# Reordering both ends of the expert loop: router on unscaled x1, selection per token tile, three early splits, the last down product pulled forward

## The chip, the cores and the metric

The kernel runs on one core of a Trainium2 chip. A core has a matrix engine (TensorE: PE for its matmuls, PEld for its weight loads), VectorE (DVE), ScalarE (ACT), GpSimd (POOL) and SyncE (SP), which here only issues DMAs. The five run their own instruction streams and meet only at semaphores: an instruction waits until a semaphore has reached a value, and another instruction's end raises it. PSUM is the accumulator memory that TensorE writes, in eight banks of 2 KB for each of 128 partitions; SBUF is the working memory. The metric is the device time of one execution in microseconds (us), lower is better, and the median over runs is compared.

## The reference, cut to what matters

One layer: attention of two kinds, a residual, then a mixture of experts with another residual. The change touches only the second half:

```python
x1 = x + concat(y_a, y_b) @ w_o                 # 512 tokens x 1024
h  = rms_norm(x1, g_ffn)                        # x1 * rsqrt(mean(x1^2) + eps) * g_ffn
logits = h @ w_router + b_router                # 32 experts
top_vals, top_idx = top_k(logits, 4)
gates = softmax(top_vals)
# for each expert e, for the tokens that chose it (at most 128 are worked on at once):
gu  = xb @ w_gu[e] + b_gu[e]                    # 1024 -> 2048
glu = min(gu[:, :1024], 7); lin = clip(gu[:, 1024:], -7, 7)
act = glu * sigmoid(1.702 * glu) * (lin + 1)
y   = (act @ w_down[e] + b_down[e]) * gate      # 1024 -> 1024
out = x1 + sum over the experts of y, each row added to its token's row
```

## The kernel before, in words

Tokens are worked on in four tiles of 128 (`T` = 4). Everything up to the router follows `PLAN`, one list of steps that every engine walks through in the same order, each doing its part of a step. In `attend(n)` the table `late` places the steps that follow a token tile's attention, by how many attention units later they come: `post` (x1 = output projection + x, DVE L1283; its squares on ACT, L965), `post_mean` and the power on POOL, `post_norm` (h2, DVE L1295), `turn_h2` (PE transposes h2 in eight 128x128 blocks, ACT and DVE copy one half each out of PSUM), `route` (eight matmuls with the router weights, then bias, maximum and index on DVE, L1308 to L1312). x1 is written to `out`, h2 to a table `hd` in device memory, both by SP.

After the plan comes the selection for all four tiles at once on DVE (L1316 to L1332): a one-hot of the four choices (`one`, 512 elements a partition), its sum over the choices (`selm`), a bf16 copy (`selb`, semaphore `picked`); PE turns it into running counts (`rank_ps`); DVE makes `rank`, each token's place in each expert's list, and `cnt`, the longest list, and then raises `routed`. `slots` (ACT L990 and L993) makes the 0/1 matrix of tokens against places for expert j as relu(1 - |place - rank|); `find` (PE) makes the list of token numbers from it, `slot_rows` (DVE) stores it as `idx`, and POOL gathers the rows of h2 with an indirect DMA (`gather`, L788) into `xg`. `spread_gates` (DVE) and `find_gates` (PE) do the same for the gates.

The expert loop computes in fp32 by splitting each number in a high and a low part and adding three products. A *chunk* is 1 MB of expert weights; each expert has eight for the first product (`NG` = 8) and four for the second (`ND` = 4). SP loads a chunk into one of eight buffers (`RAW` = 8) as soon as that buffer's last chunk has been split; `split_hi` (ACT L629) and `split_lo` (DVE L634) write its two parts to one of four places (`HL` = 4); `chunk_products` (PE L1627) runs twelve 512-column matmuls on it and raises `chunk_used`, for which the split four chunks later waits. Around them, for expert i: `turn_x` (PE transposes the gathered rows, ACT and DVE write high and low part of `xT`), `gate_up` (bias matmuls that start four PSUM banks, then eight chunks), `sigmoid` and `lin` (ACT L1026 and DVE L1383, both on those banks), `activate` (DVE L1390 and L1394, semaphore `act_ok`), `turn_a` (transposes the result, written as `aT`), `down` (bias matmuls, then four chunks), `y_rows` (ACT L1034 scales by the gates into the one buffer `ysb`), `scatter` (POOL L797, an indirect DMA that adds rows to `out`). While `gate_up(i)` runs, the work of expert i-1 is finished: PE runs `gate_up(i)`, `turn_x(i+1)`, `down(i-1)`.

The same loop body stands a second time inside `more_rounds`, for experts with more than 128 tokens. With these inputs it isn't entered, but each engine still loads `cnt` and steps three times through the loop's head before it reaches the end of the program.

The order on each engine is the order in which the code is written. The two ends that the change touches are the functions `act_round`, `dve_round`, `pe_round` and `pool_round`.

## Time and profile before

| | |
|---|---|
| median of 3 runs | 1646.47 us (1644.99 to 1647.39) |
| the profiled execution | 1646.24 us, span 1644.5 us |
| busy in that span | PE 1519.8 us (92%), DVE 1310.6 (80%), ACT 1113.0 (68%), POOL 212.8 (13%) |
| mean granted TensorE clock | 0.955 of full speed |
| matmuls of the expert chunks | 3072 + 1536 of 394 ns each |
| weight loads of the experts | 256 + 128 of 1024 KB, 7.4 and 7.0 us from issue to landing |

The span runs from the first to the last instruction; 1.7 us of the execution lie around it. The end of a matmul in the trace is modelled, and matmuls overlap, so a mean of 394 ns doesn't say how closely they follow each other; the start times of a run of matmuls do. Times named below as "at 402.4" are microseconds from the start of the span.

### The profile page before, as it was taken

How to read it: one execution, taken by the hardware profiler on the slowest of the kernel's cores; microseconds unless marked ns; L12 is line 12 of the kernel's file. 1: busy time of each engine (PE TensorE's matmuls, PEld its weight loads, DVE VectorE, ACT ScalarE, POOL GpSimd, SP SyncE). 2: the span in 40 equal slices, each digit the busy share in tenths (PEclk: the TensorE clock that was granted, in tenths of full speed). 3: DMA queues.
4: the chain of work that ended last, by engine and by line, in shares of the span. 5: the costliest groups of instructions: out<-in, count | busy, mean ns of one | idle time of the engine just before them, and what ended most of it. 6: DMA issues, size and time to landing. Idle time of an engine off the chain costs nothing.

```text
span 1644.5 us, 19287 instructions
## 1 busy us (share of the span) xinstructions
PE 1519.8 (92%) x7379; PEld 1227.3 (75%) x7382; DVE 1310.6 (80%) x1249; ACT 1113.0 (68%) x1225; POOL 212.8 (13%) x156
## 2 busy tenths in 40 slices
PE   6888668996799999999999999999999999999994
PEld 5776556775577888887887888888887888888883
DVE  4668847544599888888898888988898888888992
ACT  5544364552577777777777777777777777777771
POOL 1734301001000100001000100001000110001000
PEclk9999958996799999999999999999999999999997
DMA  6312011118579999999989999999999999999960
GB/s 186 90 52 64 1 57 47 39 39 302 186 298 355 358 357 354 359 356 363 357 333 361 360 349 350 362 354 363 360 338 353 358 352 355 354 353 363 360 254 14
DMA packets 97632, 446.62 MB, mean 272 GB/s; under 512 B 17264, under 2 KB 18416, under 8 KB 64688
## 3 DMA queue, kind: packets, MB, share of 16 engines
q1 hardware_dynamic: 87264, 428.39, 68.8%
q0 software_dynamic: 9216, 16.81, 4.0%
q8 instruction: 61, 1.00, 0.2%
q14 instruction: 51, 0.42, 0.1%
q10 hardware_dynamic: 1040, 0.00, 0.0%
HBM read 440.95 MB, written 20.97 MB: 281 GB/s over the span
## 4 chain that ended last, share of the span: by engine, by line
PE 83%; DVE 10%; ACT 3%; issue 2%; DMA 0%; POOL 0%; SPq 0%; ACTq 0%; DVEq 0%; POOLq 0%
PE ps L1627 64%; PE ps L1636 2%; PE ps L1447 2%; PE ps L1454 2%; PE ps L1448 2%; PE ps L1449 2%; PE ps L1606 2%; PE ps L1614 2%; DVE work L1191 1%; PE ps L1535 1%; PE ps L1653 1%; DVE top L1190 1%; DVE whl L634 1%; DVE rp L1148 1%; DVE ss L1127 1%
## 5 line engine op out<-in xcount | busy, mean ns | idle before, releaser
L634 DVE TENSOR_TENSOR whl<-wraw,whl 128x2048 fp32r<-128x2048 f32 x383 | 863.6, 2289 | 131.6 <-ACT whl L629 127.0
L629 ACT ACTIVATE whl<-wraw 128x2048 fp32r<-128x2048 f32 x384 | 735.8, 1917 | 243.4 <-PE ps L1627 243.3
L1627 PE MATMUL ps<-whl,xT 128*128 128x512 f32 x3072 | 726.5, 394 | 0.2 <-DVE whl L634 0.2
L1627 PEld LDWEIGHTS ps<-whl,xT 128*128 128x128 f32 x3072 | 572.5, 189 | 128.3 <-issue 11.8
L1627 PE MATMUL ps<-whl,aT 128*128 128x512 f32 x1536 | 360.3, 394 | 1.8 <-DVE aT L1376 1.8
L1627 PEld LDWEIGHTS ps<-whl,aT 128*128 128x128 f32 x1536 | 287.9, 189 | 72.3 <-issue 11.2
L797 POOL DMA_INDIRECT out_dram<-ysb,idx x32 | 74.1, 2315 | 551.5 <-ACT ysb L1034 551.5
L788 POOL DMA_INDIRECT xg<-h_rows,idx x32 | 33.6, 1051 | 560.9 <-DVE idx L1356 560.5
L1447 PE MATMUL ps<-W,HT 128*128 128x512 f32 (+1 forms) x184 | 72.7, 395 | 1.7 <-DVE HT L1103 1.7
L1448 PE MATMUL ps<-W,HT 128*128 128x512 f32 (+1 forms) x184 | 70.5, 383 | 0.0
L1449 PE MATMUL ps<-W,HT 128*128 128x512 f32 (+1 forms) x184 | 70.4, 383 | 0.0
L911 ACT ACTIVATE raw<-ps,nmax 128x256 f32<-128x256 f32 (+2 forms) x48 | 27.8, 580 | 55.6 <-DVE nmax L1204 55.6
L1204 DVE TENSOR_REDUCE nmax<-ps 128x1 f32<-128x128 f32 (+3 forms) x64 | 31.0, 487 | 31.4 <-PE ps L1513 31.0
L1026 ACT ACTIVATE acts<-ps 128x1024 f32<-128x1024 f32 x32 | 32.8, 1024 | 31.0 <-PE ps L1627 31.0
L990 ACT ACTIVATE ohd<-iota,rank 128x128 bf16<-128x128 f32 x128 | 40.4, 386 | 8.3 <-DVE cnt L1332 8.3
L473 POOL TENSOR_TENSOR W<-WR,W 128x1024 fp32r<-128x1024 f32 x16 | 38.2, 2388 | 59.4 <-ACT W L837 59.3
L1454 PE MATMUL ps<-ident,stk 128*128 128x128 f32 x168 | 28.7, 324 | 18.6 <-DVE stk L1167 12.1
L1034 ACT ACTIVATE ysb<-ps,gslot 128x1024 f32<-128x1024 f32 x32 | 35.1, 1096 | 15.6 <-PE ps L1627 15.6
L1636 PE MATMUL ps<-bgs,sel_gu 64*128 64x512 f32 x128 | 40.3, 436 | 4.5 <-DVE acts L1394 4.5
L1383 DVE TENSOR_SCALAR acts<-ps 128x1024 f32<-128x1024 f32 x32 | 38.8, 1214 | 5.4 <-PE ps L1627 5.4
L1447 PEld LDWEIGHTS ps<-W,HT 128*128 128x128 f32 x184 | 36.7, 199 | 8.1 <-DVE HT L1103 2.0
L1449 PEld LDWEIGHTS ps<-W,HT 128*128 128x128 f32 x184 | 36.1, 196 | 6.8
(219 smaller groups left out, 1490.4 us busy)
## 6 DMA issues: line engine op xcount, KB each, us to landing
wraw<-in_w_gu_dram SPq DMA_DIRECT2D x256, 1024.0 KB, 7.4
wraw<-in_w_down_dram SPq DMA_DIRECT2D x128, 1024.0 KB, 7.0
WR<-in_w_in_dram SPq DMA_DIRECT2D x20, 512.0 KB, 3.6
WR<-in_w_o_dram SPq DMA_DIRECT2D x8, 512.0 KB, 3.6
xs<-in_x_dram SPq DMA_DIRECT2D x4, 512.0 KB, 5.8
WR<-in_x_dram SPq DMA_DIRECT2D x4, 512.0 KB, 4.1
out_dram<-WR SPq DMA_DIRECT2D x4, 512.0 KB, 2.6
h_rows<-WR SPq DMA_DIRECT2D x4, 512.0 KB, 2.6
```

Source lines behind the costliest of these rows:

```text
L473: eng.tensor_tensor(b[:, 1], piece(m), b[:, 0].bitcast(F32), ALU.subtract).then_inc(w_lo, 1)
L629: act.activation(whl[:, n % HL, 0, :], wraw[n % RAW], ACT.Copy).then_inc(chunk_hi, 1)
L634: eng.tensor_tensor(whl[:, n % HL, 1, :], wraw[n % RAW], whl[:, n % HL, 0, :].bitcast(F32), ALU.subtract).then_inc(chunk_lo, 1)
L797: pool.indirect_dma_start(out[0], bass.IndirectOffsetOnAxis(ap=idx[:, e:e + 1], axis=0), ysb, None, bounds_check=SEQ - 1, oob_is_err=False ...
L990: ins = act.activation(ohd[:, t, :], iota, ACT.Abs, bias=rank[:, t, j:j + 1], scale=-1.0)
L1383: dve.tensor_scalar(acts[:, 1, :].rearrange("p (a n) -> p a n", a=2), ps[:, GU + 2:GU + 4, :], LIMIT + 1.0, 1.0 - LIMIT, ALU.min, ALU.max) ...
L1447: pe.matmul(dst, a[0], b[0], start=k_first, stop=False)
L1448: pe.matmul(dst, a[0], b[1], start=False, stop=False)
L1449: return pe.matmul(dst, a[1], b[0], start=False, stop=k_last)
L1454: ins = pe.transpose(tbank(g)[:, j * P:(j + 1) * P], s_, ident)
L1627: ins = pe.matmul(bank, a[x_][j], w[:, b, j, 512 * q:512 * q + 512], start=False, stop=last and j == nj - 1 and n == 2)
L1636: ins = pe.matmul(bank, sel_gu, bgs[:, 512 * q:512 * q + 512], start=True, stop=False)
```

## The change

In the plan, the PE transposes x1 itself instead of h2, two units earlier in the chain (`turn_x1` in the place of `turn_h2`), and the router follows one unit earlier. The gain `g_ffn` is multiplied into the router weights once, in the setup step (a second small strided load on ACT's queue fetches it), and the factor 1/rms is applied to the logits together with the bias. h2 is still computed for the table `hd`. The selection's one-hot, sum and copy are made per token tile inside `route`; the full `one` is made later, in `spread_gates`. `cnt` is computed after the first two lists (semaphore `counted`). The slots of experts 0 and 1 are made by DVE with a compare in the place of ACT's two functions. The low split of chunk 1 moves from POOL to DVE. The bias matmuls of expert 0 come before its rows are turned, the gates after. Expert 1's first three splits come ahead of expert 0's `sigmoid` and `lin`. At the end `turn_a(31)` runs inside `down(30)`, its result goes to `xT` and `down(31)` accumulates in the gate/up banks. The wait for the last scatter moves from POOL to SP, behind SP's pass through the loop's head.

```diff
     late = {-5: ["mix_b"], -3: ["mix_norm"], 3: ["mix_a"], 4: ["turn_y"], 13: ["post"],
-            14: ["post_mean"], 15: ["post_norm"], 16: ["turn_h2"], 17: ["route"]}
+            14: ["turn_x1", "post_mean"], 15: ["post_norm"], 16: ["route"]}
...
+LEAD = 3
...
+        def a_of(e):
+            return xT if e == E - 1 else aT
+        def dn_bank(e):
+            return GU if e == E - 1 else DN
...
@@ more_rounds, sync
+            eng.wait_ge(counted, 1)
             most = eng.value_load(cnt[0:1, 0:1], min_val=0, max_val=SEQ)
...
             more_rounds(sp, stream)
+            sp.wait_ge(scattered, 16 * E)
@@ gpsimd
-            pool.wait_ge(chunk_lo, 1)
-            split_lo(pool, 0, 0, 1)
...
-                after(pool, passed_ok, 2 * E * r)
-                pool.wait_ge(scattered, 16 * (E * r + E))
+                if not is0(r):
+                    pool.wait_ge(passed_ok, 2 * E * r)
+                    pool.wait_ge(scattered, 16 * (E * r + E))
@@ scalar
+            act.dma_start(gfcol, g_ffn[0].rearrange("(k p) -> p k", p=P), allow_slow_non_contiguous=True) \
+               .then_inc(gfcol_in, 16)
...
             def act_round(r):
-                slots(r, 0)
-                slots(r, 1)
...
+                for c in range(LEAD):
+                    split_hi(act, r, 1, c)
                 sigmoid(r, 0)
...
-                    for c in range(NG):
+                    for c in range(LEAD if i == 1 else 0, NG):
                         split_hi(act, r, i, c)
...
-                for c in range(NG, NCH):
-                    split_hi(act, r, E - 1, c)
+                pick_dn(r, E - 1)
+                split_hi(act, r, E - 1, NG)
+                split_hi(act, r, E - 1, NG + 1)
+                turn_a_hi(r, E - 1)
+                split_hi(act, r, E - 1, NG + 2)
                 y_rows(r, E - 2)
-                pick_dn(r, E - 1)
-                turn_a_hi(r, E - 1)
+                split_hi(act, r, E - 1, NG + 3)
                 y_rows(r, E - 1)
@@ vector, setup and route
+                    dve.tensor_tensor(wrt, wrt, gfcol.unsqueeze(2).to_broadcast([P, KD, E]), ALU.mult) \
+                       .then_inc(wrt_ok, 1)
...
-                    dve.tensor_tensor(lg[:, t, :], ps[:, ACC, 0:E], brt, ALU.add).then_inc(logit_ok, 1)
+                    dve.scalar_tensor_tensor(out=lg[:, t, :], in0=ps[:, ACC, 0:E], scalar=tss[:, 2:3], in1=brt,
+                                             op0=ALU.mult, op1=ALU.add).then_inc(logit_ok, 1)
...
+                    link(dve.tensor_copy(idxf[:, t, :], idx8[:, t, 0:TOPE]))
+                    link(dve.tensor_tensor(one_t, iota[:, 0:E].unsqueeze(1).to_broadcast([P, TOPE, E]),
+                                           idxf[:, t, :].unsqueeze(2).to_broadcast([P, TOPE, E]), ALU.is_equal))
+                    link(dve.tensor_reduce(selm[:, t, :], one_t.rearrange("p k e -> p e k"), AX.X, ALU.add))
+                    dve.tensor_copy(selb[:, t, :], selm[:, t, :]).then_inc(picked, 1)
...
+            def first_slots(r, j):
...
+                for t in range(T):
+                    ins = dve.tensor_scalar(oh[:, j, t, :], iota, rank[:, t, j:j + 1], None, ALU.is_equal)
+                ins.then_inc(slots_ok, 1)
@@ vector, dve_round
+                first_slots(r, 0)
+                first_slots(r, 1)
                 slot_rows(r, 0)
                 slot_rows(r, 1)
                 if is0(r):
+                    most_rows()
                     spread_gates()
+                    split_lo(dve, 0, 0, 1)
+                turn_x_lo(r, 0)
                 slot_gates(r, 0)
                 slot_gates(r, 1)
...
+                for c in range(LEAD):
+                    split_lo(dve, r, 1, c)
                 lin(r, 0)
+                activate(r, 0)
                 turn_x_lo(r, 1)
-                activate(r, 0)
...
-                for c in range(NG, NCH):
-                    split_lo(dve, r, E - 1, c)
+                split_lo(dve, r, E - 1, NG)
+                split_lo(dve, r, E - 1, NG + 1)
                 turn_a_lo(r, E - 1)
+                split_lo(dve, r, E - 1, NG + 2)
+                split_lo(dve, r, E - 1, NG + 3)
@@ tensor
-                    pe.wait_ge(h2_ok, t + 1)
+                    pe.wait_ge(x1_ok, t + 1)
...
-            pe.wait_ge(picked, 1)
+            pe.wait_ge(picked, T)
...
             def turn_x(r, j):
-                pe.wait_ge(gslot_ok, E * r + min(j + 2, E))
+                if j:
+                    pe.wait_ge(gslot_ok, E * r + min(j + 2, E))
...
             def down(r, e):
...
-                after(pe, yrow_ok, E * r + e)
+                if e == E - 1:
+                    pe.wait_ge(act_ok, E * r + E)
+                else:
+                    after(pe, yrow_ok, E * r + e)
...
+                    if e == E - 2 and c == NG + 1:
+                        turn_a(r, E - 1)
@@ tensor, pe_round
-                find_gates(r, 0)
-                find_gates(r, 1)
                 if is0(r):
                     pe.wait_ge(bg_ok, 2)
+                gate_up_bias(r, 0)
+                pe.wait_ge(counted, 1)
                 turn_x(r, 0)
+                for j in range(2):
+                    pe.wait_ge(idx_ok, E * r + j + 1)
+                    find_gates(r, j)
...
-                turn_a(r, E - 1)
                 down(r, E - 1)
```

How the order moves, at three places. First VectorE at the router of the last token tile, before; the first row is x1, `wraw_67,whl` is the low split of chunk 0, `lg` the logits:

```order
L1283 TENSOR_TENSOR WR<-ps,WR 128x1024 [waits rows_out,xres_in,acc_ps]
L1288 TENSOR_SCALAR tss<-tss 128x1 [waits x1_sq]
L1295 SCALAR_TENSOR_TENSOR WR<-WR,tss,rel 128x1024 [waits x1_root]
L1301 COPY WR<-ps 128x512 [waits turned]
L634 TENSOR_TENSOR whl<-wraw_67,whl 128x2048 [waits chunk_hi]
L1308 TENSOR_TENSOR lg<-ps,brt 128x32 [waits logit_ps]
L1311 MAX top_122<-lg 128x8 [waits logit_ok]
L1312 MAX_INDEX idx_123<-top_122,lg 128x8 [waits dve_step]
L1316 TENSOR_TENSOR gate<-top_122 128x16 [waits dve_step]
L1318 CAST idxf<-idx_123 128x16
L1319 TENSOR_TENSOR one<-iota,idxf 128x512 [waits dve_step]
L1323 TENSOR_REDUCE selm<-one 128x128 [waits dve_step]
```

and now, from the same row on:

```order
L1303 TENSOR_TENSOR WR<-ps,WR 128x1024 [waits rows_out,xres_in,acc_ps]
L1321 COPY WR<-ps 128x512 [waits turned]
L1308 TENSOR_SCALAR tss<-tss 128x1 [waits x1_sq]
L1315 SCALAR_TENSOR_TENSOR WR<-WR,tss,rel 128x1024 [waits x1_root]
L647 TENSOR_TENSOR whl<-wraw_67,whl 128x2048 [waits chunk_hi]
L1328 SCALAR_TENSOR_TENSOR lg<-ps,tss,brt 128x32 [waits logit_ps]
L1332 MAX top_124<-lg 128x8 [waits logit_ok]
L1333 MAX_INDEX idx_125<-top_124,lg 128x8 [waits dve_step]
L1334 CAST idxf<-idx_125 128x4 [waits dve_step]
L1335 TENSOR_TENSOR one_t<-iota,idxf 128x128 [waits dve_step]
L1337 TENSOR_REDUCE selm<-one_t 128x32 [waits dve_step]
L1338 CAST selb<-selm 128x32 [waits dve_step]
```

The copy of the turned half stands ahead of the mean, and the one-hot and its sum are a quarter as large.

Second, VectorE where expert 0 ends and expert 1 begins, before (`xT` here is the low part of expert 1's rows, the two `acts` with SCALAR_TENSOR_TENSOR are `activate(0)`):

```order
L1383 TENSOR_SCALAR acts<-ps 128x1024 [waits chunk_used]
L1368 TENSOR_TENSOR xT<-ps,xT 128x512 [waits xT_hi] x2
L1390 SCALAR_TENSOR_TENSOR acts<-acts 128x1024 [waits lin_ok,sig_ok]
L1394 SCALAR_TENSOR_TENSOR acts<-ps,acts 128x1024 [waits prod_ok]
L634 TENSOR_TENSOR whl<-wraw_67,whl 128x2048 [waits chunk_hi]
L634 TENSOR_TENSOR whl<-wraw_68,whl 128x2048 [waits chunk_hi]
L634 TENSOR_TENSOR whl<-wraw_69,whl 128x2048 [waits chunk_hi]
```

and now:

```order
L647 TENSOR_TENSOR whl<-wraw_67,whl 128x2048 [waits chunk_hi]
L647 TENSOR_TENSOR whl<-wraw_68,whl 128x2048 [waits chunk_hi]
L647 TENSOR_TENSOR whl<-wraw_69,whl 128x2048 [waits chunk_hi]
L1416 TENSOR_SCALAR acts<-ps 128x1024 [waits chunk_used]
L1423 SCALAR_TENSOR_TENSOR acts<-acts 128x1024 [waits lin_ok,sig_ok]
L1427 SCALAR_TENSOR_TENSOR acts<-ps,acts 128x1024 [waits prod_ok]
L1401 TENSOR_TENSOR xT<-ps,xT 128x512 [waits xT_hi] x2
```

The three splits stand ahead of everything that waits for expert 0's last chunk, and the activation ahead of expert 1's rows.

Third, TensorE at the last two experts, before, from the second chunk of `down(30)` on:

```order
L1627 MATMUL ps<-whl,aT 128x512 [waits chunk_lo]
L1627 MATMUL ps<-whl,aT 128x512 x11
L1627 MATMUL ps<-whl,aT 128x512 [waits chunk_lo]
L1627 MATMUL ps<-whl,aT 128x512 x11
L1614 MATMUL ps<-ident,acts 128x128 [waits act_ok]
L1614 MATMUL ps<-ident,acts 128x128 x7
L1653 MATMUL ps<-bgs,sel_dn 128x512 [waits yrow_ok,sel_ok]
L1653 MATMUL ps<-bgs,sel_dn 128x512
L1627 MATMUL ps<-whl,aT 128x512 [waits chunk_lo,aT_lo]
L1627 MATMUL ps<-whl,aT 128x512 x11
```

and now:

```order
L1654 MATMUL ps<-ident,acts 128x128 [waits act_ok]
L1654 MATMUL ps<-ident,acts 128x128 x7
L1667 MATMUL ps<-whl,aT 128x512 [waits chunk_lo]
L1667 MATMUL ps<-whl,aT 128x512 x11
L1667 MATMUL ps<-whl,aT 128x512 [waits chunk_lo]
L1667 MATMUL ps<-whl,aT 128x512 x11
L1701 MATMUL ps<-bgs,sel_dn 128x512 [waits act_ok,sel_ok]
L1701 MATMUL ps<-bgs,sel_dn 128x512
L1667 MATMUL ps<-whl,xT 128x512 [waits chunk_lo,aT_lo]
L1667 MATMUL ps<-whl,xT 128x512 x11
```

The transposes of the last activation stand two chunks earlier, and the last bias matmuls no longer wait for `yrow_ok`, the reading of the banks of expert 30.

## Rows read from the trace of the kernel before

**Rows 1.** Windows: busy us by engine, clock, DMA share, in two stretches.

```profile
core 0: us, PE busy (x) PEld busy (x) DVE busy (x) ACT busy (x) POOL busy (x), PEclk, DMA share, GB/s
397.00:425.00 28.00, 10.14 (x72) 8.16 (x70) 19.49 (x34) 11.61 (x19) 8.89 (x5) 0.50 0.55 190
...
569.00:606.00 37.00, 37.00 (x179) 29.71 (x179) 32.89 (x22) 28.86 (x25) 3.38 (x2) 1.00 0.93 355
```

**Rows 2.** Timeline, router: start, us, engine, operation [idle before <-releaser].

```profile
392.61 1.06 ACT L965 ACTIVATE WR<-WR 128x1024 f32<-128x1024 f32 x1 [10.77 <-DVE WR L1283]
...
394.61 1.28 DVE L1295 SCALAR_TENSOR_TENSOR WR<-WR,tss,rel 128x1024 f32<-128x1024 f32 x1 [0.66 <-POOL tss L770]
...
402.42 0.19 DVE L1308 TENSOR_TENSOR lg<-ps,brt 128x32 f32<-128x32 f32 x1 [1.58 <-PE ps L1564]
...
402.67 0.95 POOL L774 MEMSET xg<- 128x1024 f32 x1 [8.10 <-DVE lg L1308]
...
403.27 0.39 DVE L1318 CAST idxf<-idx 128x16 f32<-128x16 uint32 x1
...
403.58 4.49 POOL L634 TENSOR_TENSOR whl<-wraw,whl 128x2048 fp32r<-128x2048 f32 x1
403.69 4.94 DVE L1319 TENSOR_TENSOR one<-iota,idxf 128x512 f32<-128x512 f32 x1
...
408.66 1.02 DVE L1323 TENSOR_REDUCE selm<-one 128x128 f32<-128x512 f32 x1
...
411.86 1.28 ACT L990 ACTIVATE ohd<-iota,rank 128x128 bf16<-128x128 f32 x4 [8.26 <-DVE cnt L1332]
```

**Rows 3.** Timeline 415 to 425, from the first gather to the first product.

```profile
415.48 1.29 POOL L788 DMA_INDIRECT xg<-h_rows,idx  x1 [6.51 <-DVE idx L1356]
...
416.92 0.69 DVE L1340 TENSOR_TENSOR onek<-one,gate 128x512 f32<-128x512 f32 x1
...
420.84 2.29 DVE L634 TENSOR_TENSOR whl<-wraw,whl 128x2048 fp32r<-128x2048 f32 x1
...
421.02 1.94 PE L1606 MATMUL ps<-ident,xg 128*128 128x128 f32 x8 [0.30 <-issue]
...
424.90 18.87 PE L1627 MATMUL ps<-whl,xT 128*128 128x512 f32 x72
```

**Rows 4.** Instructions of the gather, L788, 400 to 470.

```profile
DMA to landing us min/median/max: 4.2/4.9/5.6
```

**Rows 5.** Timeline 455 to 476, expert 1 begins.

```profile
455.02 2.04 PE L1636 MATMUL ps<-bgs,sel_gu 64*128 64x512 f32 x4 [4.53 <-DVE acts L1394]
...
457.22 4.50 PE L1627 MATMUL ps<-whl,xT 128*128 128x512 f32 x12 [0.16 <-DVE whl L634]
...
462.36 13.89 PE L1627 MATMUL ps<-whl,xT 128*128 128x512 f32 x60
```

**Rows 6.** Timeline 1594 to 1629, the last two experts.

```profile
1594.67 11.18 PE L1627 MATMUL ps<-whl,aT 128*128 128x512 f32 x48
...
1599.34 11.09 DVE L634 TENSOR_TENSOR whl<-wraw,whl 128x2048 fp32r<-128x2048 f32 x5
...
1609.64 2.21 POOL L797 DMA_INDIRECT out_dram<-ysb,idx  x1 [33.42 <-ACT ysb L1034]
...
1611.68 13.93 PE L1627 MATMUL ps<-whl,aT 128*128 128x512 f32 x48 [1.83 <-DVE aT L1376]
...
1627.54 1.55 POOL L797 DMA_INDIRECT out_dram<-ysb,idx  x1 [15.69 <-ACT ysb L1034]
```

**Rows 7.** Instructions that touch out_dram, 1600 to 1646.

```profile
DMA to landing us min/median/max: 6.4/6.7/7.0
```

**Rows 8.** POOL queue at lines L639 and L216: durations ns, start.

```profile
L639 POOLq TENSOR_LOAD <-cnt x1: 512/512/512, 1634.0 to 1634.0; - x1
...
L216 POOLq DRAIN  x1: 5302/5302/5302, 1639.0 to 1639.0; - x1
```

**Rows 9.** DMA queues, 0 to 12: packets, MB, share of 16 engines.

```profile
q10 hardware_dynamic: 1040, 0.00, 4.8%
```

101 lines of the change are left out of this document (55 added, 46 removed).

## The prediction

> **What bounds the kernel now.** I read the busy windows first. In the middle of the expert loop TensorE is busy in all of a 37 us stretch while VectorE is busy 32.9, ScalarE 28.9 and the DMA engines 0.93 of it [rows 1]: the loop is TensorE's, and an order that only moves splits inside it gives nothing. From the first product at 424.90 to the last down product at 1611.68 there are 32 expert periods of 37.1 us [rows 3, 6]. What the change can win lies where TensorE waits: between 397 and 425 it is busy 10.1 of 28 us, at a granted clock of 0.50 [rows 1], and after 1606. So I read the timeline there, from one releaser to the next.
>
> Router: x1 is ready at 392.6, h2 is written from 394.61 for 1.28, the logits are read at 402.42, the compare for the one-hot takes 4.94, its sum 1.02, and ScalarE starts the slots at 411.86 when `cnt` is there [rows 2]. Then the gather starts at 415.48, the gates are spread on VectorE, TensorE turns the gathered rows at 421.02 and the first product starts at 424.90 [rows 3]. End: `down(30)` takes 11.18 for 48 matmuls, VectorE splits five chunks from 1599.34 to 1610.43 and only then writes the last activation's low part, so `down(31)` starts at 1611.68 and takes 13.93 for the same 48 [rows 6]. The last scatter is issued at 1627.54 and lands 6.4 later [rows 6, 7]; POOL then loads `cnt` at 1634.0, steps through the loop's head until 1639.0 and drains for 5.3 us [rows 8], to the end of the span.
>
> **The change part by part**, on the clock of the execution before, x1 at 392.6.
>
> *Router, up to the slots.* The PE turns x1 at once, beside ScalarE's squares (1.06). VectorE's copy of a half (bounded by 1.28 for twice the elements, taken 0.7) now stands ahead of the mean, so h2 starts at 395.3 and ends at 396.6. The low split of chunk 0 (2.29, the price at 420.84) still follows, to 398.9. The logits are ready by then, since their turn starts three microseconds earlier; the router is read at 398.9 in the place of 402.42: 3.5 won. Maximum, index and cast stay. The one-hot is a quarter of a compare whose kind costs 0.69 undisturbed at 512 elements (416.92), so 0.25; the sum a quarter of 1.02, 0.3. Before, logits to `picked` took 7.5 (402.42 to 409.9, which is 408.66 + 1.02 and a copy); I count 2.2, to 401.1. Why the compare took 4.94: POOL's split ran from 403.58 to 408.07, the compare from 403.69 to 408.63 [rows 2]. That split goes to VectorE (2.29), behind the gates. Ranks: counts, clearing, `rank` and `cnt` took 1.9 (409.9 to 411.86), now 1.3, the clearing done earlier and `cnt` later: slots start at 402.4, not 411.86, 9.4 won.
>
> The Trainium skill, SBUF — State Buffer, section "SBUF: two separate sides", says that VectorE and GpSimd share a port pair as an exclusive lock for a whole instruction, and that a VectorE operation with two SBUF inputs is held only by a GpSimd operation that reads SBUF. The trace agrees: 4.94 beside a POOL split and 0.69 alone. By that rule the POOL clearing of `xg`, 0.95 long, would not hold the small compare that now runs beside it; were it held as the cast at 403.27 seems to be (0.39, ending with the clearing), the chain would be 0.7 longer.
>
> *Slots to first product.* Eight compares on VectorE replace two times 1.28 and the relu behind them; each is 128 elements, I take 0.13, 1.0 together. The first list is then stored at about 403.7 and the gather starts 1.0 later (as 415.48 did after its list) at 404.7. It lands in 4.2 to 5.6 [rows 4]; I take the median 4.9: 409.6. Turning the rows 1.94; behind it the last half's high and low copies and the start took 1.94 before (422.96 to 424.90) and do again: first product at 413.4. The other chain, on VectorE, is `cnt`, the gates (3.9 from 416.92 to 420.84 plus 0.6 before it, plus 0.7 for `one`) and the split of chunk 1: 403.7 + 0.4 + 5.2 + 2.3 = 411.6, hidden by the gather. The expert 0 bias (about 2.0 at half clock, as at 455.02) is done while the gather flies. So the first product comes 11.5 earlier. Bounds: 12.7 with the shortest landing and slots at no cost; 9.0 if the slots cost twice that, the landing is 5.6 and the clearing holds the compare.
>
> *Three early splits.* Before, expert 1's first product at 457.22 waited 0.16 for its split, and the next 60 matmuls ran without a stop, 13.89 [rows 5]. TensorE's gap is the 4.53 before 455.02, released by `activate(0)` [rows 5], and that the splits don't shorten: the third can only start when chunk 6 has been used, about 2.8 before the last, needs 1.9 on ScalarE and 2.3 on VectorE, and so delays `lin` by 1.4; the activation ahead of `turn_x_lo` gives 1.3 back. Sum 0.1 won, bounds -1.5 and +2.
>
> *Last down product.* `turn_a(31)` stands behind the second chunk of `down(30)`, at 1600.3, after the activation, which ends as the splits begin at 1599.34: no wait. Of the five splits (2.2 each), three come first, to 1606.0, then the low part (1.3): 1607.4. TensorE ends `down(30)` and the turn at 1606.6, bias 0.5, and starts the product at 1607.5, with a gap too short for the clock to fall: 11.18 in the place of 13.93. End of the products 1618.7, not 1625.6: 6.9 won. The read of expert 31 needs the scatter of 30 landed, since both use `ysb`: that starts at about 1608.8 (1609.64 before) and lands 6.4 to 7.0 later, 1615.8 [rows 6, 7]. Bounds 5.0 (one more split on the chain) and 7.3.
>
> *End of the program.* POOL no longer waits for the landing: `cnt` and the loop's head (1634.0 to 1639.0) run while the scatter flies, the drain starts at issue + 6.6 in the place of + 11.5, and SP sees the landing at + 6.4. With the drain of 5.3 [rows 8] unchanged, 4.9 won. The trace shows this drain only once, so the bounds are wide: 0, if it ends by the scatter and not by its own length, and 9.9, if it shrinks to nothing and the landing alone is left.
>
> The Trainium skill, VectorE: DVE Perf Modes, section "The DRAIN you can't avoid", calls the drains of the program's frame constant and about 12 ns on every engine. The trace has 5302 ns on POOL and doesn't agree; taken at its word, the 5.3 us would be a wait for something else and the change would win either end of the bounds.
>
> *Costs.* Four small operations per tile, about 0.9 us on VectorE, now lie inside attention for tiles 0 to 2, where VectorE releases TensorE part of the time: I take 0.9 for two tiles, nothing for the third, and 0.8 back, as TensorE waits for x1 and not for h2. Bounds -1 and +3. The second strided load beside x: the first takes 4.8% of 16 engines over 12 us [rows 9], 0.6 us; I take 0.3. One small multiply in the setup is hidden behind the first projection.
>
> Sum: 11.5 + 0.1 + 6.9 + 4.9 - 1.2 = 22.2. From the profiled execution of 1646.24: 1624.0. The median shown, 1646.47, is 0.2 above that execution, within the runs' spread, so the forecast stands at 1624.0.
>
> **The rivals.**
> 1. *The drain eats the end.* The drain is long because something that the scatter starts takes that long, and it ends where it did after the issue. For it: 5.3 us on one engine only. Against it: it began 5 us after the landing. 22.2 - 4.9 = 17.3: 1628.9.
> 2. *The drain goes too.* It was a cost of having waited, and the end comes with the landing: 4.9 to 5.0 more, 1619.1.
> 3. *The front gives less.* The gather lands later, with chunks 6 and 7 still loading beside it, or the selection inside attention is exposed in every tile: 4 less, 1628.0.
> 4. *The three splits do pay.* Expert 1 starts with a full ring and the 4.53 gap closes. Against it the order of `lin` behind the third split. 4.0 more: 1620.0.
> 5. *Slower.* The loop stops being TensorE's: entered 11.5 us earlier, with the rows of `hd` and the first chunks closer together, the loads fall behind and never catch up, since the DMA engines are at 0.93 [rows 1]. It decides from 22.2 / 31 = 0.72 us on each of the 31 following periods, that is from 37.8 up; at 38.0 the time is 1646.2 - 22.2 + 31 x 0.9 = 1651.9. Against it: a load is asked for eight chunks, 24.7 us, before it is needed.
>
> **How the numbers follow.** Forecast 0.62, its own range 1620 to 1628 by the bounds of the front and of the last product. Rival 1 0.13, rival 2 0.09, rival 3 0.08, rival 4 0.05, rival 5 0.03. Range 1617.0 to 1631.5: it takes in rivals 1 to 4 with two microseconds of the front's bounds on either side. A measurement of this kernel tells 0.2%, 3.3 us, from no change; all cases but rival 5 are faster by more, so faster 0.96, same 0.01, slower 0.03.
>
> **What would show it.** Right: logits read about 6 us after x1 is ready, and the compare at 0.2 to 0.3; first product 20.8 us after x1 (32.3 before); the gap ahead of expert 1's bias still 4 to 5; periods of 37.1; the last 48 products in 11.2, directly behind `down(30)`; the drain starting before or with the landing. Wrong: a gather that lands 7 us after issue, a period above 37.1, a gap of more than a microsecond ahead of the last product, or a drain of another length. The forecast fails if the end of the program is tied to the scatter by more than the landing, or if attention grows by more than 3 us.

## The result and the profile after

The changed kernel takes 1623.02 us (median of 4 runs, 1621.51 to 1626.04) against 1646.93 us for the kernel before beside it. The ratio is 0.9861, with a 95% interval from 0.9848 to 0.9873. The forecast was 1624.0 us, with a range from 1617.0 to 1631.5. The profiled execution took 1624.25 us with a span of 1622.5. That span is 22.0 us shorter than the one of before.

The router first. This is VectorE's timeline from x1 of the last tile on (start, duration, engine, line, operation, what it writes and reads, and in brackets the idle time and what ended it):

```profile
395.60 1.22 DVE L1303 TENSOR_TENSOR WR<-ps,WR 128x1024 f32<-128x1024 f32 x1 [6.69 <-PE ps L1487]
...
402.83 0.24 DVE L1328 SCALAR_TENSOR_TENSOR lg<-ps,tss,brt 128x32 f32<-128x32 f32 x1
...
403.64 0.47 DVE L1334 CAST idxf<-idx 128x4 f32<-128x4 uint32 x1
404.14 0.29 DVE L1335 TENSOR_TENSOR one_t<-iota,idxf 128x128 f32<-128x128 f32 x1
404.47 0.37 DVE L1337 TENSOR_REDUCE selm<-one_t 128x32 f32<-128x128 f32 x1
404.88 0.39 DVE L1338 CAST selb<-selm 128x32 bf16<-128x32 f32 x1
...
406.50 1.66 DVE L1383 TENSOR_SCALAR oh<-iota,rank 128x128 bf16<-128x128 f32 x8
...
415.73 1.30 DVE L1401 TENSOR_TENSOR xT<-ps,xT 128x512 fp32r<-128x512 f32 x2
```

And POOL and TensorE in the same stretch:

```profile
403.14 0.95 POOL L789 MEMSET xg<- 128x1024 f32 x1 [3.74 <-DVE lg L1328]
404.28 0.95 POOL L792 MEMSET xg<- 128x1024 f32 x1 [0.19 <-DMA h_rows<-WR]
409.21 1.29 POOL L801 DMA_INDIRECT xg<-h_rows,idx  x1 [3.98 <-DVE idx L1389]
```

```profile
408.52 2.07 PE L1676 MATMUL ps<-bgs,sel_gu 64*128 64x512 f32 x4
413.73 1.94 PE L1646 MATMUL ps<-ident,xg 128*128 128x128 f32 x8 [3.15 <-DMA xg<-h_rows,idx]
...
417.08 3.35 PE L1667 MATMUL ps<-whl,xT 128*128 128x512 f32 x7 [1.22 <-DVE xT L1401]
```

x1 is ready at 395.60 + 1.22 = 396.82, and the first product starts at 417.08. That is 20.3 us, where the kernel before took 32.3 [rows 2, 3]. The compare that answers to the one of 4.94 [rows 2] takes 0.29. The release of the first product is still the copy of the gathered rows, and behind that the gather: TensorE waited 3.15 us for it with the biases already done. Before, the same biases stood between the turn of the rows and the first product, and ended with it:

```profile
422.89 2.07 PE L1636 MATMUL ps<-bgs,sel_gu 64*128 64x512 f32 x4
```

The low copy of the rows was done at about 424.3 then, 0.6 ahead of the product; now the product follows the copy. So the last leg, from the start of the turn to the first product, is 3.4 us in the place of 3.9.

The end, TensorE, VectorE and POOL:

```profile
1585.99 5.74 PE L1667 MATMUL ps<-whl,aT 128*128 128x512 f32 x24
1591.57 1.04 PE L1654 MATMUL ps<-ident,acts 128*128 128x128 f32 x8
...
1598.02 0.73 PE L1701 MATMUL ps<-bgs,sel_dn 64*128 64x512 f32 x2
1598.68 11.17 PE L1667 MATMUL ps<-whl,xT 128*128 128x512 f32 x48
```

```profile
1590.65 6.68 DVE L647 TENSOR_TENSOR whl<-wraw,whl 128x2048 fp32r<-128x2048 f32 x3
1597.25 1.28 DVE L1409 TENSOR_TENSOR xT<-ps,xT 128x512 fp32r<-128x512 f32 x2
```

```profile
1611.78 1.55 POOL L810 DMA_INDIRECT out_dram<-ysb,idx  x1 [9.62 <-ACT ysb L1049]
```

The two products stand back to back; from the start of `down(30)` to the end of the last product it is 23.9 us, where it was 30.9 [rows 6]. The queues' own rows at the end (durations in ns as least/median/most, then first and last start) answer to [rows 8]:

```profile
L653 POOLq TENSOR_LOAD <-cnt x1: 515/515/515, 1611.6 to 1611.6; - x1
```

```profile
L217 POOLq DRAIN  x1: 5302/5302/5302, 1617.0 to 1617.0; - x1
...
L217 SPq DRAIN  x1: 7/7/7, 1618.5 to 1618.5; - x1
```

POOL's queue loads `cnt` at 1611.6 and runs its empty loop beside the scatter's own 1.55 us on POOL. The drain is as long as before, to the nanosecond, and begins 1.5 us ahead of the moment at which SP, which waits for the landing, gets to its own. From the issue of the last scatter to the end it is 10.7 us, where it was 17.0 (1627.54 [rows 6] to 1644.5).

The loop between the two ends is TensorE's as before (busy time of the engines in a 37 us stretch, granted clock, DMA share), compare [rows 1]:

```profile
569.00:606.00 37.00, 37.00 (x179) 29.73 (x179) 32.90 (x22) 28.77 (x26) 3.38 (x2) 1.00 0.95 358
```

### The profile page after: what moved, and what is told of

Its sections match the earlier page's. It is cut to its first block, busy times and chain, and to the rows that moved or that the text cites. A ratio compares the mean times of both kernels' runs of the same rounds, so it can differ in the third digit from the quotient of the medians.

```text
span 1622.5 us, 19298 instructions
## 1 busy us (share of the span) xinstructions
PE 1516.4 (93%) x7379; PEld 1225.1 (76%) x7382; DVE 1312.7 (81%) x1272; ACT 1109.0 (68%) x1215; POOL 209.4 (13%) x155
## 4 chain that ended last, share of the span: by engine, by line
PE 84%; DVE 9%; ACT 3%; issue 2%; DMA 0%; POOL 0%; SPq 0%; POOLq 0%; ACTq 0%; DVEq 0%
PE ps L1667 66%; PE ps L1676 2%; PE ps L1492 2%; PE ps L1485 2%; PE ps L1487 2%; PE ps L1486 2%; PE ps L1654 2%; PE ps L1646 2%; PE ps L1573 1%; PE ps L1701 1%; DVE work L1208 1%; DVE top L1207 1%; DVE rp L1165 1%; DVE ss L1144 1%; ACT W L853 1%
## 5 line engine op out<-in xcount | busy, mean ns | idle before, releaser
L1667 PE MATMUL ps<-whl,xT 128*128 128x512 f32 x3120 | 736.9, 394 | 1.2 <-DVE xT L1401 1.2
L1667 PEld LDWEIGHTS ps<-whl,xT 128*128 128x128 f32 x3120 | 580.8, 189 | 130.7 <-issue 11.6
L1667 PE MATMUL ps<-whl,aT 128*128 128x512 f32 x1488 | 346.7, 392 | 0.0
L1667 PEld LDWEIGHTS ps<-whl,aT 128*128 128x128 f32 x1488 | 276.8, 188 | 67.5 <-issue 11.2
L1221 DVE TENSOR_REDUCE nmax<-ps 128x1 f32<-128x128 f32 (+3 forms) x64 | 30.9, 486 | 33.0 <-PE ps L1551 32.7
L1492 PEld LDWEIGHTS ps<-ident,stk 128*128 128x128 f32 x168 | 23.4, 168 | 24.6 <-DVE stk L1184 15.1
L1401 DVE TENSOR_TENSOR xT<-ps,xT 128x512 fp32r<-128x512 f32 x64 | 40.7, 675 | 0.0
```

The costliest lines, as they stand in the source:

```text
L1401: dve.tensor_tensor(xT[:, 1, 4 * b:4 * b + 4, :], ps[:, TP + b, :].rearrange("p (k n) -> p k n", k=4), xT[:, 0, 4 * b:4 * b + 4, :].bitcas ...
L1492: ins = pe.transpose(tbank(g)[:, j * P:(j + 1) * P], s_, ident)
L1667: ins = pe.matmul(bank, a[x_][j], w[:, b, j, 512 * q:512 * q + 512], start=False, stop=last and j == nj - 1 and n == 2)
```

## The experiments

Twelve kernels ran. The executions of one kernel lie 1.5 to 5.5 us apart, and the interval on a ratio is 2 to 3 us to either side, so differences under 2.5 us are taken from the profiles and not from the medians. A profile is one execution, and where its stretches vary by themselves this is said. "Change" below is the ratio to the kernel before, less 0.9861, times 1646.9. The three last columns, in us, are read from the timeline of each kernel's one profiled execution: "attention" runs from x1 of tile 0 to x1 of tile 3 ready, "front" from there to the first product, "end" from the issue of the last scatter to the end of the span.

| kernel | median us | ratio, 95% | change us | attention | front | end |
|---|---|---|---|---|---|---|
| before | 1646.9 | 1 | | 114.8 | 32.3 | 17.0 |
| changed | 1623.0 | 0.9861 (0.9848 to 0.9873) | 0 | 120.6 | 20.3 | 10.7 |
| e1 POOL waits | 1629.9 | 0.9901 (0.9884 to 0.9917) | +6.6 | 118.0 | 20.3 | 16.7 |
| e2 tail order back | 1629.9 | 0.9900 (0.9883 to 0.9916) | +6.4 | 117.9 | 20.3 | 10.6 |
| e3 no early splits | 1625.4 | 0.9875 (0.9858 to 0.9891) | +2.3 | 118.0 | 20.2 | 10.4 |
| e4 turn one later | 1621.9 | 0.9853 (0.9836 to 0.9869) | -1.3 | 117.4 | 20.3 | 10.5 |
| e5 one branch | 1623.6 | 0.9851 (0.9835 to 0.9868) | -1.6 | 117.9 | 21.0 | 9.2 |
| e6 selection at the end | 1622.7 | 0.9850 (0.9834 to 0.9867) | -1.8 | 114.2 | 23.3 | 10.6 |
| e9 turn as before | 1626.3 | 0.9870 (0.9854 to 0.9887) | +1.5 | 121.2 | 20.3 | 10.3 |
| e8 gain later | 1623.1 | 0.9858 (0.9843 to 0.9873) | -0.5 | 117.8 | 20.4 | 10.3 |
| f1 selection in a wait | 1619.4 | 0.9836 (0.9823 to 0.9849) | -4.1 | 114.4 | 20.3 | 10.5 |
| c1 four edits | 1618.2 | 0.9830 (0.9817 to 0.9843) | -5.1 | 114.7 | 20.3 | 9.3 |
| before + end alone (b1) | 1639.2 | 0.9944 (0.9928 to 0.9961) | | 117.8 | 32.3 | 10.3 |
| before + split alone (b2) | 1643.3 | 0.9981 (0.9972 to 0.9990) | | 114.7 | 29.8 | 17.2 |

**e1: POOL waits for the last scatter again.**

```diff
                 if not is0(r):
                     pool.wait_ge(passed_ok, 2 * E * r)
-                    pool.wait_ge(scattered, 16 * (E * r + E))
+                pool.wait_ge(scattered, 16 * (E * r + E))
...
-            sp.wait_ge(scattered, 16 * E)
```

> The changed kernel with one part undone: POOL waits again for the last scatter to land before it loads cnt and runs the loop's head; SP's wait is gone. Theory A (the loop's head and the drain of 5.3 us have lengths of their own and start when POOL's queue gets there): from the issue of the last scatter to the end 17.0 us instead of 10.7, 1623.0 + 6.2 = 1629.2. Rival (the drain ends with something that the scatter starts, so where POOL waits is nothing): 1623.0, the drain shorter.

It came so: 6.6 by the ratio, and 16.7 us from issue to end. The queue's row of e1 shows the drain unchanged, 11.2 us behind the issue of the scatter at 1609.52:

```profile
L217 POOLq DRAIN  x1: 5302/5302/5302, 1620.7 to 1620.7; - x1
```

**b1: the same part alone on the kernel before**, the reverse edit of e1.

> The kernel before with the end of the program alone changed: POOL doesn't wait for the last scatter, SP does. Theory A: from the issue of the last scatter to the end 10.5 to 10.7 us in the place of 17.0, 1646.9 - 6.2 = 1640.7. Rival (the 6.2 hang on the new order of the last products): less than 3, above 1644. Its attention is that of the kernel before, so it shows how far the time from x1 of tile 0 to x1 of the last tile (114.8 us in the one profile of before, 118 to 120.6 in four of the changed kernel's program) moves from one execution to the next: if the loss is the change's, about 115; if it is chance, 115 to 118.

The end takes 10.3 us there too, so this part is worth 6.6 without any of the others; by the ratio it is 9.2 (6.4 to 11.9), whose lower end just takes it in. The second result is the attention: 117.8 us with instructions that are those of before, where two other executions of them (before, b2) show 114.8 and 114.7. The same instructions took 3 us more in one execution of three, so one profile alone doesn't settle 3 us there.

**e5: one branch over the empty loop.**

```diff
-            with eng.Fori(1, ROUNDS) as r:
-                with eng.If(most > r * P):
-                    one_round(r)
-                eng.nop()
+            with eng.If(most > P):
+                with eng.Fori(1, ROUNDS) as r:
...
```

> The changed kernel with one branch more: each engine steps over the whole loop of later rounds when cnt is at most 128, in the place of three empty turns through it. In the changed kernel POOL loads cnt at 1611.6, needs 4.4 us for the three empty turns and drains for 5.3 from 1617.0. Theory A (the drain has its own length and starts when the queue gets there): the drain starts 3 to 4 us earlier, the end 3 us earlier, and then the landing of the last scatter (6.4 to 7.0 after its issue) is next to set the end, 8 to 8.5 us after the issue in the place of 10.5: 1620.5. Rival (the drain can't end before the scatter's own work has ended plus a fixed time): the drain gets longer by what it starts earlier, 1623.0.

Neither theory holds as written. The end takes 9.2 us, 1.1 to 1.5 less than the 10.3 to 10.7 of the kernels with the loop. The one branch still costs 2.8 us, from 1615.6 to the drain at 1618.4, and the drain became longer, 5488 ns:

```profile
L654 POOLq COMPARE_BRANCH  x1: 53/53/53, 1615.6 to 1615.6; - x1
```

```profile
L217 POOLq DRAIN  x1: 5488/5488/5488, 1618.4 to 1618.4; - x1
```

That one branch costs nearly as much as the loop agrees with the loop's rows in the changed kernel. The test that steps over the body first runs at 1612.5, the count at the loop's end first at 1615.5, so 3.0 of the 4.4 us lie in the first turn and 1.4 in the two others and the way out. Why the first step over the body is slow isn't shown:

```profile
L655 POOLq COMPARE_BRANCH  x3: 50/50/53, 1612.5 to 1616.6; - x3
```

```profile
L654 POOLq ALU_OP  x3: 32/32/49, 1615.5 to 1616.8; - x3
```

For the drain, SP's last row, which comes 0.2 us behind the landing (e4: issue at 1608.63, landing 6.4 later, row at 1615.2), gives the key (e5; then c1, where the scatter was issued at 1607.81; then e2, at 1616.45):

```profile
L217 SPq DRAIN  x1: 7/7/7, 1621.4 to 1621.4; - x1
```

```profile
L222 POOLq DRAIN  x1: 5907/5907/5907, 1611.0 to 1611.0; - x1
...
L222 SPq DRAIN  x1: 7/7/7, 1614.4 to 1614.4; - x1
```

```profile
L217 POOLq DRAIN  x1: 5575/5575/5575, 1621.2 to 1621.2; - x1
...
L217 SPq DRAIN  x1: 7/7/7, 1624.3 to 1624.3; - x1
```

In these three the drain ends 2.5 us behind SP's row (1623.9, 1616.9 and 1626.8), 2.7 behind the landing. In the other kernels with SP's wait it has 5302 ns, and its end lies 3.3 us or more behind that row by itself, as 1622.3 against 1618.5 in the changed kernel. So one rule fits all fourteen profiles: the drain ends at the later of two times, its start + 5.3 and the landing + 2.7. It is read from three executions and not from a run made for it, and since SP waits for the landing in all three, they can't tell whether the drain goes by the landing or by SP's arrival. By this rule the one branch wins what it won here and no more.

The front of this profile, 21.0 us, is no effect of the branch that can be seen: its gather landed 5.3 us after its issue (409.15 to 414.44), where the changed kernel's took 4.5.

**e2: the tail's order back.**

```diff
-            return xT if e == E - 1 else aT
+            return aT
...
-            return GU if e == E - 1 else DN
+            return DN
...
-                    if e == E - 2 and c == NG + 1:
-                        turn_a(r, E - 1)
...
+                turn_a(r, E - 1)
                 down(r, E - 1)
```

and on ScalarE and VectorE the four splits of the last expert all ahead of its activation's halves, on ScalarE the rows of expert 30 (`y_rows`) and then `pick_dn` too.

> The changed kernel with the last down product's order undone: the last activation is turned behind down(30), its halves are written behind all splits, into aT, and the banks are DN again. Theory A (the wait for the low half, 4.3 us of gap and 2.7 for a product that starts at half clock): start of down(30) to the end of down(31) 30.9 instead of 23.9, 1623.0 + 7.0 = 1630.0. Rival (the scatter of 30 or ScalarE's rows would set the end anyway): under 3 us, below 1626.

Measured +6.4. TensorE shows the two gaps and the slower product, VectorE the five splits ahead of the low half:

```profile
1584.16 11.18 PE L1660 MATMUL ps<-whl,aT 128*128 128x512 f32 x48
...
1598.60 0.90 PE L1691 MATMUL ps<-bgs,sel_dn 64*128 64x512 f32 x2 [2.39 <-ACT sel_dn L1015]
1601.17 13.35 PE L1660 MATMUL ps<-whl,aT 128*128 128x512 f32 x48 [1.67 <-DVE aT L1404]
```

```profile
1588.83 11.09 DVE L647 TENSOR_TENSOR whl<-wraw,whl 128x2048 fp32r<-128x2048 f32 x5
1599.84 1.28 DVE L1404 TENSOR_TENSOR aT<-ps,aT 128x512 fp32r<-128x512 f32 x2
```

From 1584.16 to 1614.52 are 30.4 us against 23.9: 6.5, of which 2.2 are the clock (13.35 for 11.17) and the rest the gap.

**e3: `LEAD = 0`.**

> The changed kernel with LEAD = 0: no split of expert 1 stands ahead of the activation of expert 0; the activation still stands ahead of the low halves of the gathered rows. Theory A (TensorE waits there for the activation, not for splits): the idle time ahead of expert 1's bias stays at 4 to 4.6 us, the next 60 products may start up to 0.5 later; 1623.0, within 0.7. Rival (the early splits pay for themselves): 1625 to 1627.

By the profiles it lies between the two. (The median, 1625.4, is in the rival's range, but the intervals don't tell +2.3 from 0.) The gap ahead of the bias is shorter without the splits, 3.13 us, since the activation no longer stands behind the third; but then the first product waits for its split, and twelve products take 5.46 us at a granted clock of 0.50 (from 442 to 450), where they take 4.31 in the changed kernel, whose clock comes back at about 451, while they run:

```profile
442.26 2.04 PE L1676 MATMUL ps<-bgs,sel_gu 64*128 64x512 f32 x4 [3.13 <-DVE acts L1427]
445.65 5.46 PE L1667 MATMUL ps<-whl,xT 128*128 128x512 f32 x12 [1.35 <-DVE whl L647]
```

```profile
446.92 2.04 PE L1676 MATMUL ps<-bgs,sel_gu 64*128 64x512 f32 x4 [4.62 <-DVE acts L1427]
448.90 4.31 PE L1667 MATMUL ps<-whl,xT 128*128 128x512 f32 x12
```

(the second fence is the changed kernel). From the first product of all to the bias of `down(0)` e3 takes 58.2 us, the ten kernels with the early splits 56.6 to 58.8, and the kernel before 58.0. Part of this is how soon the clock comes back behind the first product (the first 72 products take 18.0 us in e3, 18.4 in the changed kernel, 19.4 in e5). From the turn of expert 1's rows to that bias it is 34.4 in e3, 32.9 to 33.1 in nine kernels with the splits, 33.6 in e5 and 33.5 before. So the early splits are worth 0.8 to 1.5 us, on one profile of e3.

**b2: the POOL split alone moved, on the kernel before.**

```diff
-            pool.wait_ge(chunk_lo, 1)
-            split_lo(pool, 0, 0, 1)
...
-                    dve.wait_ge(chunk_lo, 2)
+                    split_lo(dve, 0, 0, 1)
                     split_lo(dve, 0, 0, 2)
```

> The kernel before with the low split of chunk 1 of expert 0 alone moved from POOL to VectorE, behind the gates. Theory (VectorE's compare was held by POOL's split): the compare of 512 elements takes 0.7 in the place of 4.94, the slots start 4.3 earlier, 2.3 of it is given back to the split that now stands on VectorE ahead of the first product: 1646.9 - 2.0 = 1644.9. Rival (that compare is slow by its own inputs): 4.94 stays, and the split costs up to 2.3: 1647 to 1649. Its attention is again that of the kernel before: x1 of tile 0 to x1 of tile 3 was 114.8 and 117.8 us in two executions.

The same compare on the same 512 elements now takes 0.69 us, and the front 29.8 in the place of 32.3: 2.5 won, 3.1 by the ratio (1.6 to 4.6).

```profile
403.36 0.39 DVE L1316 CAST idxf<-idx 128x16 f32<-128x16 uint32 x1
403.78 0.69 DVE L1317 TENSOR_TENSOR one<-iota,idxf 128x512 f32<-128x512 f32 x1
```

```profile
402.77 0.95 POOL L774 MEMSET xg<- 128x1024 f32 x1 [8.10 <-DVE lg L1306]
403.66 0.98 POOL L777 MEMSET xg<- 128x1024 f32 x1
```

The second clearing runs from 403.66 to 404.64, over the whole compare (403.78 to 404.47), and doesn't hold it; beside POOL's split, which reads SBUF, it took 4.25 us longer [rows 2]. The cast ahead of it is held: it ends at 403.75 with the first clearing (403.72).

**e4, e9: where x1 of tiles 0 to 2 is turned.** e4 moves the turn from lag 14 to 15, e9 the turn to 16 and the router to 17, where they stood before; the last tile stays as changed. The edit of e9:

```diff
+    early = {**late, 14: ["post_mean"], 16: ["turn_x1"], 17: ["route"]}
...
-            for kind in {**late, -5: [], -3: [], 1: ["mix_b"], 3: ["mix_norm", "mix_a"]}.get(lag, []) \
-                    if t == 0 else late.get(lag, []):
+            for kind in {**early, -5: [], -3: [], 1: ["mix_b"], 3: ["mix_norm", "mix_a"]}.get(lag, []) \
+                    if t == 0 else (early if t < T - 1 else late).get(lag, []):
```

> The changed kernel with x1 of tiles 0 to 2 turned one step of the plan later (lag 15 in the place of 14, the mean stays at 14); the last tile as it was. x1 of the last tile is ready 4.3 us later in the changed kernel than before. Theory A (the turn of x1 stands in TensorE's queue ahead of products that are ready, waits there for x1, and the clock falls for longer): most of it comes back, x1 of the last tile 2.5 to 3.5 us earlier, 1620.0. Rival B (the four small operations per tile on VectorE cost it): nothing moves, 1623.0. Rival C (it is lost ahead of tile 0's x1): nothing moves either, and the starts of tile 0 show it.

> The changed kernel with the turn and the router of tiles 0 to 2 where they stood before (turn at lag 16, router at lag 17; x1 is what is turned), the last tile as changed. With the turn alone one step later (the run before this) the stretch at half clock behind tile 0's x1 stayed at 17 us. Theory A (it is the order of TensorE's work there that keeps the clock low): the stretch behind 276 shortens to about 11 us as before, from x1 of tile 0 to x1 of tile 2 it takes 84 to 86 us in the place of 88.5 to 90.8, and 1620. Rival (the clock there falls and rises by itself, or the small operations on VectorE cost the time): 88 us or more, 1622 to 1623.

The turn does wait for x1 in TensorE's queue, but only for 1.1 us (at 276.27 in the changed kernel), and moving it gives back nothing that can be told from chance. The old place gives nothing back either: 121.2 us of attention, about as much as the changed kernel's profile, and +1.5 by the ratio, inside the noise. From x1 of tile 0 to x1 of tile 2 it took 90.8 us, and the stretch at half clock was 24 us long (275 to 299), not 11. Theory A, that this order keeps the clock low, fell.

**e8: the gain's load behind the squares**, the `dma_start` of `gfcol` moved behind ScalarE's loop over x.

> The changed kernel with the strided load of the gain (gfcol) issued behind ScalarE's squares of x in the place of ahead of them. In the changed kernel the rows of x land 0.6 later and VectorE's first operation is at 11.07, not 10.37. Theory A (the strided load takes the DMA engines from x): 10.4 again, 0.7 won if nothing else takes it: 1622.3. Rival (that time is made good later anyway: x1 of tile 0 is ready no later than before, 276.2 against 277.8): 10.4, and the same time, 1623.0.

VectorE's first operation came at 10.71, between the two values (10.37 before, 11.07 in the changed kernel), and the time stayed: -0.5 by the ratio, with the interval on both sides of zero. x1 of tile 0 is ready at 276.1 to 278.9 in all fourteen profiles, with the load at the start or without it. No cost of the start can be seen.

**e6 and f1: the selection of tiles 0 to 2.** In e6 its four operations stand with those of the last tile, behind x1. In f1 they stand in VectorE's wait for the last output projection:

```diff
                 elif kind == "post":
                     t = st[1]
+                    for u in range(T - 1) if t == T - 1 else ():
+                        select(u)
                     dve.wait_ge(acc_ps, t + 1)
```

> The changed kernel with the four small operations of the selection (cast, compare, sum, cast) of tiles 0 to 2 done with those of the last tile. Rival B (they cost attention its time): x1 of the last tile 2.5 us or more earlier than in the four profiles of the same program part so far (394.1 to 396.8), say 391.5; the router then has 3 x 1.1 = 3.3 us more. Theory A (the order on TensorE and its clock cost it): x1 of the last tile where it was, 394 to 396, and the time 1623.0 + 3.3 = 1626.3.

> The changed kernel with the four small operations of the selection of tiles 0 to 2 moved into VectorE's wait for the last output projection, ahead of x1 of the last tile (it idles 4.5 to 6.7 us there; they need 3 x 1.1 = 3.3). With them behind x1 (the run e6) x1 of the last tile was ready at 391.45, 114.2 us behind that of tile 0, and the router paid 3.0. Theory B (inside tiles 0 to 2 they cost attention about 3 us): from x1 of tile 0 to x1 of tile 3 114 to 115.5 us, from there to the first product 20.3 as in the changed kernel, 1623.0 - 3.0 = 1620.0. Rival (the short attention of e6 was chance, as the same program part has lain between 117.9 and 120.6): 117.5 or more, 1623.0.

Both show 114.2 and 114.4 us of attention, where the six executions with the selection inside (changed, e1, e2, e3, e5, e8) show 117.8 to 120.6. e6 gives it back in the router (23.3 for 20.3), f1 doesn't: 1619.4 us, -4.1. The medians agree: e6 less the 3.0 of its router is 1619.7, c1 (below) plus the 1.2 by which its end is shorter 1619.4, both against 1623.0. VectorE's rows of f1, where the wait used to be:

```profile
386.30 0.17 DVE L1111 CAST idxf<-idx 128x4 f32<-128x4 uint32 x1
...
387.25 0.18 DVE L1115 CAST selb<-selm 128x32 bf16<-128x32 f32 x1
...
390.73 1.23 DVE L1312 TENSOR_TENSOR WR<-ps,WR 128x1024 f32<-128x1024 f32 x1 [1.22 <-PE ps L1493]
```

Three selections fit, and 1.22 us of the wait are left. Where the time goes is seen from x1 of one tile to x1 of the next, in us, with the mean granted clock of the stretch in brackets:

| | tile 0 to 1 | 1 to 2 | 2 to 3 | sum | of it at half clock |
|---|---|---|---|---|---|
| before and b2 | 41.3, 41.2 (0.90) | 43.0 (1.00) | 30.4 (0.83) | 114.8, 114.7 | 18.5 |
| b1, the same instructions | 44.4 (0.81) | 43.0 (1.00) | 30.4 (0.83) | 117.8 | 27 |
| changed | 44.5 (0.81) | 44.0 (1.00) | 32.1 (0.79) | 120.6 | 30 |
| e1 and e3 | 45.5, 45.6 (0.78) | 44.0 (1.00) | 28.5, 28.4 (0.94) | 118.0 | 23 |
| e2, e5, e8 | 44.5 to 44.6 (0.79) | 46.2 (0.93) | 27.1 (1.00) | 117.8 to 117.9 | 25 |
| e6 and f1: selection outside | 44.1 (0.81) | 43.0 (1.00) | 27.1, 27.2 (1.00) | 114.2, 114.4 | 17 |
| c1: selection outside | 44.1 (0.79) | 42.5 (1.00) | 28.1 (0.94) | 114.7 | 22 |

The last column is worked out from the others: a mean of 0.90 over 41.3 us is 8.3 us at half clock, as the clock has only the two levels. The selection inside costs 1.0 us in the second stretch at an undisturbed clock (44.0 for 43.0). The rest of the 3.5 stands in stretches whose clock differs too: the six executions with it inside have 23 us or more at half clock, e6 and f1 17, c1 22. Within one column the stretch is longer where the clock is lower (27.1 at 1.00, 28.4 at 0.94, 32.1 at 0.79). So the twelve small operations, 1.1 us a tile, cost about 1.2 us a tile on average, but only part of that is seen apart from the clock. That they cause the longer half clock, through TensorE's waits for VectorE, is argued and not shown.

**c1: f1, e4, e5 and e8 together.**

> The changed kernel with four edits together: the selection of tiles 0 to 2 in VectorE's wait (f1), x1 of tiles 0 to 2 turned one step later (e4), one branch over the loop (e5) and the gain's load behind the squares (e8). If the parts add: 1623.0 - 3.0 - 1.1 - 1.4 - 0.7 = 1616.8. Rival (the parts in attention are chance and only the end of the program is left): 1621.6.

1618.2 us, ratio 0.9830 (0.9817 to 0.9843): 1.2 below f1, as much as its end is shorter in the profile (9.3 for 10.5). Of the two other edits nothing can be seen. f1 and c1 are both faster than the changed kernel; which of the two is faster, the intervals don't tell.

## Why the prediction was right, step by step

The forecast was 1.0 us above the median, and 0.3 us below the profiled execution. Its sum was 22.2 us; the profiled span gives 22.0: x1 of tile 0 came 1.6 earlier, attention took 5.8 more, the front gave 12.1, the stretch from the first product to the bias of `down(30)` 0.9, the last two experts up to the scatter 7.0, and the end 6.2.

That the number is so near is luck in part. The largest miss is the cost inside attention: 1.0 was forecast, with 3 as the upper bound and a growth of more than 3 us as a sign of failing, and it came out at 3.2 against the usual execution of the kernel before and at 5.8 in the profiles compared. The front, expert 1's begin and the end each gave more than forecast and paid for it. With those as forecast the time would have been about 1626.

| term | forecast | measured | by |
|---|---|---|---|
| x1 to the first product | 11.5 | 12.1 | 32.32 - 20.26, profiles; 20.2 to 20.4 in nine kernels |
| begin of expert 1 | 0.1 | 0.3 (0.1 to 0.6) | from the turn of expert 1's rows to the bias of `down(0)`: 33.5 before (b2 33.2), 33.1 changed (32.9 to 33.1 in nine kernels) |
| last down product | 6.9 | 6.5 to 7.1 | e2, profile |
| end of the program | 4.9 | 6.2 to 6.6 | profile, e1, b1 |
| attention and start | -1.2 | -3.2 against the usual execution; -5.8 + 1.6 = -4.2 in the profiles compared | profiles; b1 and b2 for the spread |

*Router, up to the slots.* The logits were read 6.0 us after x1 (forecast 6.3), the slots started 9.7 after it (9.8), and the gather 12.4 (12.1). The reason given for the compare of 4.94 is shown by b2. The rule of the Trainium skill, SBUF — State Buffer, section "SBUF: two separate sides", gave the right answer for the compare on both counts: no hold by a clearing, a hold by a split. The forecast used only its half on operations with two SBUF inputs. The casts have one: the cast to `idxf` takes 0.47 beside the clearing and 0.17 in f1, the cast to `selb` 0.39 and 0.18, and each ends with its clearing. That is 0.5 us in the chain which the forecast didn't have. The same sentence of that section also has a VectorE operation in a 2-port mode held by a GpSimd operation, whether that reads SBUF or not; whether these two casts ran in such a mode no run shows.

*Slots.* Eight compares took 1.66, not 1.0; only the first four stand ahead of the first list, so 0.3 of it counted. The gather landed in 4.5 us (forecast 4.9), inside the bounds. The last leg was taken as before, 1.94 for the turn and 1.94 behind it, and took 3.4: the biases, which stood in it before, were already done. Hence 20.3 and not 20.8. Of the 12.1 won in the front only the 2.5 of the moved split are isolated by a run (b2); the rest is read from the timelines before and after.

*Three early splits.* The delay was as put: with them the activation comes 1.5 later (forecast 1.4, e3 3.13 against 4.62). What was missing on the other side: without them, but with the activation moved forward, the first product waits 1.35 for its split at a granted clock of 0.50, and its twelve products take 1.15 longer. Rival 4, that the gap of 4.53 closes and 4.0 us are won, is refuted by the gap of 4.62 and by e3.

*Last down product.* As put: no wait at `turn_a(31)`, the low part at 1597.25 directly behind three splits, the scatter of 30 landed in time.

*End of the program.* The mechanism was as put, the size was off by 1.3. The step that failed is "the drain starts at issue + 6.6": it started at issue + 5.2, because POOL's queue doesn't stand still while the scatter's own 1.55 us run. It loaded `cnt` 0.2 us ahead of the start of that work. Rival 2 is refuted, the drain went nowhere. Rival 1 is refuted for the changed kernel, where the drain had its own 5302 ns; what it said, that the scatter holds the drain, would by the rule from e5, c1 and e2 begin 1.3 us further down. The Trainium skill, VectorE: DVE Perf Modes, section "The DRAIN you can't avoid", puts the frame's drains at 12 ns on every engine; the runs show 7 to 81 ns on four engines and 5.3 to 5.9 us on POOL.

*Costs.* This is the term that was mis-sized: "0.9 for two tiles, nothing for the third, and 0.8 back". (With the 0.3 of the start its items add up to 1.3, and 1.2 was written.) With the selection inside, attention takes 118.0 us (median of six), without it 114.2 to 114.7 (e6, f1, c1). So the twelve small operations cost about 3.5 us, where 1.8 was put. Of the 3.5 only 1.0 stands in a stretch at full clock in both orders; the rest goes with a longer time at half clock, which no term of the forecast covered. Against two of the three executions of the kernel before, the first stretch is 2.8 us longer even with the selection outside (clock 0.81 for 0.90), and the last 2.3 to 3.2 shorter (0.94 to 1.00 for 0.83), where "0.8 back" was put. What in the change does either is open. Together the net is 3.2 against the usual execution of before, 0.2 against b1. The profiled execution of the changed kernel was the longest of the six, 120.6, so that its trace alone would have given 5.8. Rival 3 had this case, the selection exposed in every tile, for 4 us less; its cost came about, and its time of 1628.0 did not, since the other terms gave more.

Why that one execution is longer still goes with the granted clock ahead of the last output projection. The changed kernel, and then e2, which has the same instructions up to there (columns: busy time of PE, PEld, DVE, ACT, POOL with their counts, granted clock, DMA share, GB/s):

```profile
378.00:382.00 4.00, 1.97 (x8) 1.56 (x8) 1.97 (x4) 1.19 (x2) 0.00 (x0) 0.50 1.04 367
382.00:386.00 4.00, 3.76 (x9) 3.05 (x10) 1.17 (x3) 2.76 (x1) 0.00 (x0) 0.50 1.02 424
```

```profile
378.00:382.00 4.00, 1.36 (x12) 1.01 (x10) 2.31 (x5) 1.08 (x2) 0.00 (x0) 1.00 1.00 236
382.00:386.00 4.00, 4.00 (x18) 3.29 (x19) 1.16 (x2) 2.77 (x1) 0.00 (x0) 1.00 1.03 426
```

The start, for which 0.3 stood in the sum, shows no cost (e8).

*Slower, rival 5.* The periods stayed at 37.1 and the loads at their pace: from the first product to the bias of `down(30)` it is 1168.2 us, 1169.1 before. Rival 5 didn't occur.
